# All eight gate columns of the first attention branch ahead of the attention stream

## What is computed

```python
proj = einsum('bld,de->ble', rmsnorm(x, attn_norm_w), w_in)
a_q, a_k, a_v, i_q, i_k, i_w, b_q, b_k, b_v, g_a, g_b = split(proj)
o_a = dsa_branch(...)      # each query attends to the 128 causal keys that an index picks
o_b = swa_branch(...)      # sliding window of 128 keys, with a sink logit per head
mix = sigmoid(g_a) * (o_a @ w_branch_a) + sigmoid(g_b) * (o_b @ w_branch_b)
x = x + mix @ w_out
```

## Time and profile before

| | us |
|---|---|
| three runs, median | 1595.26 |
| three runs, lowest and highest | 1594.77, 1597.05 |
| the profiled execution, its own time | 1593.72 |
| its span in the trace | 1591.9 |

### The profile page before, as it was taken

How to read it: one execution, slowest core, us unless ns; L and a number is a source line. 1 busy time by engine, 2 the same in 40 slices (tenths; PEclk the granted TensorE clock), 3 DMA queues, 4 the chain that set the end, 5 groups by cost and what they waited for, 6 DMA issues and landing times.

```text
span 1591.9 us, 19579 instructions
## 1 busy us (share of the span) xinstructions
PE 1578.1 (99%) x7590; PEld 1294.2 (81%) x7590; DVE 768.6 (48%) x1106; ACT 506.2 (32%) x749; POOL 709.0 (45%) x273
## 2 busy tenths in 40 slices
PE   9999999999999999999999999999999999999998
PEld 6887788888888988888888887876678988888886
DVE  6701588910165566666104389987573431023203
ACT  3012211210125444344124344237543432124312
POOL 5875189677771344544442002421143244344451
PEclk9999999999999999999999999999999999999999
DMA  6242032232333233233223222231123122323221
GB/s 220 85 133 79 1 112 80 80 129 83 106 106 106 81 105 105 80 105 106 84 101 114 79 82 80 81 79 28 28 106 133 54 81 105 106 80 106 106 88 71
DMA packets 123285, 147.00 MB, mean 92 GB/s; under 512 B 5143, under 2 KB 98375, under 8 KB 123208
## 3 DMA queue, kind: packets, MB, share of 16 engines
q1 hardware_dynamic: 121334, 141.05, 28.2%
q10 hardware_dynamic: 1874, 4.85, 0.9%
HBM read 143.79 MB, written 2.10 MB: 92 GB/s over the span
## 4 chain that ended last, share of the span: by engine, by line
PE 95%; POOL 2%; issue 1%; ACT 1%; DVE 1%; DMA 0%; SPq 0%; DVEq 0%; POOLq 0%; ACTq 0%
PE ps L646 29%; PE ps L647 28%; PE ps L648 28%; PE ps L788 3%; PE ps L865 2%; PE ps L1032 1%; PE ps L1049 1%; POOL w_lo L599 1%; PE ps L853 1%; POOL w_hi L594 1%; PE ps L924 1%; PE ps L886 0%; DMA raw<-in_w_up 0%; POOL spare_lo_out L599 0%; PE ps L826 0%
## 5 line engine op out<-in xcount | busy, mean ns | idle before, releaser
L599 POOL TENSOR_TENSOR w_lo<-raw,w_hi 128x1024 fp32r<-128x1024 f32 x224 | 557.4, 2509 | 714.9 <-ACT w_hi L1094 712.2
L646 PE MATMUL ps<-hT_hi,w_hi 128*128 128x512 f32 (+1 forms) x928 | 355.7, 383 | 0.8 <-POOL w_lo L599 0.5
L647 PE MATMUL ps<-hT_lo,w_hi 128*128 128x512 f32 (+1 forms) x928 | 354.4, 382 | 0.0
L648 PE MATMUL ps<-hT_hi,w_lo 128*128 128x512 f32 (+1 forms) x928 | 354.3, 382 | 0.0
L1094 ACT ACTIVATE w_hi<-raw 128x2048 fp32r<-128x2048 f32 (+1 forms) x87 | 165.0, 1896 | 246.5 <-PE ps L646 212.3
L646 PEld LDWEIGHTS ps<-hT_hi,w_hi 128*128 128x128 f32 x928 | 174.4, 188 | 37.0 <-issue 2.3
L648 PEld LDWEIGHTS ps<-hT_hi,w_lo 128*128 128x128 f32 x928 | 174.4, 188 | 33.7
L647 PEld LDWEIGHTS ps<-hT_lo,w_hi 128*128 128x128 f32 x928 | 174.5, 188 | 33.5
L594 POOL TENSOR_TENSOR w_hi<-raw,cells 128x2048 fp32r<-128x2048 f32 x35 | 130.1, 3716 | 127.7 <-PE ps L646 126.0
L648 PE MATMUL ps<-w_hi,f_lo 128*128 128x512 f32 x400 | 155.6, 389 | 0.0
L646 PE MATMUL ps<-w_hi,f_hi 128*128 128x512 f32 x400 | 155.6, 389 | 0.0
(11 more groups left out here) (306 smaller groups left out, 2188.3 us busy)
## 6 DMA issues: line engine op xcount, KB each, us to landing
raw<-in_w_in SPq DMA_DIRECT2D x86, 512.0 KB, 4.6
raw<-in_w_up SPq DMA_DIRECT2D x76, 512.0 KB, 4.6
raw<-in_w_down SPq DMA_DIRECT2D x54, 512.0 KB, 4.1
raw<-in_w_out SPq DMA_DIRECT2D x16, 512.0 KB, 4.3
raw<-in_w_ret_o SPq DMA_DIRECT2D x8, 512.0 KB, 4.1
raw<-in_w_sgu_o SPq DMA_DIRECT2D x8, 512.0 KB, 4.1
x<-in_x SPq DMA_DIRECT2D x4, 512.0 KB, 6.0
raw<-in_w_branch_b SPq DMA_DIRECT2D x4, 512.0 KB, 6.2
```

Source lines behind the costliest of these rows:

```text
L599: nc.gpsimd.tensor_tensor(lo[:, c], raw[:, s, c], hi[:, c].bitcast(f32), ALU.subtract).then_inc(unit_split, 1)
L646: first = nc.tensor.matmul(dst, a_hi, b_hi, start=start, stop=False)
L647: nc.tensor.matmul(dst, a_hi, b_lo, start=False, stop=False)
L648: return first, nc.tensor.matmul(dst, a_lo, b_hi, start=False, stop=stop)
```

## The change

`GA_IN` goes from 7 to 8. So `GA_PARTS` is 0, the stream's first four parts are gone, and the parts of `y_b` are numbered from 0; they stay in the same steps. The eighth `g_a` column is made ahead of the stream and evacuated as a sigmoid. `y_b`'s first unit gets its high part after the sixth sigmoid. The late sigmoid is gone.

```diff
-GA_IN = 7
+GA_IN = 8
...
-HI_AT = {1: U0["y_b"], GA_PARTS + 1: U0["y_b"] + 1, GA_PARTS + 9: U0["y_a"]}
+HI_AT = {1: U0["y_b"] + 1, 9: U0["y_a"]}
...
             for j in range(GA_IN // 2):
                 unit_T(U0["g_a"] + j, T0["g_a"] + 2 * j, KT, 256, hT_hi, hT_lo)
-            column(U0["g_a"] + 3, G_A[6], KT, 256, 0, hT_hi, hT_lo)
...
                 evacuate(G_A[c], sig_a[:, c, :], ACT.Sigmoid)
-                if c in (1, 3):
+                if c in (1, 3, 5):
                     give_hi(U0["g_a"] + c // 2 + 2, started=True)
...
-            nc.scalar.activation(sig_a[:, GA_IN:KT, :], sig_a[:, GA_IN:KT, :], ACT.Sigmoid).then_inc(sigmoids_made, 1)
             give_hi(U0["y_a"] + 1, started=True)
```

## The result

The changed kernel takes **1600.87 us** in the median of 12 runs (1596.60 to 1602.13), the kernel before 1595.98 in 12 (1594.19 to 1597.60): a ratio of 1.0029, interval 1.0021 to 1.0036. It is slower by 0.3%, some 4.9 us. The forecast was 1595.7 and the range ended at 1599.5: it missed, on the side of rivals A and B.

The account below looks back on a forecast made before the run. TensorE, busy 99% of the span, was taken to bound the kernel. The terms 5.44 - 5.52 - 1.2 + 1.7 gave +0.4 us on the median of 1595.26, so 1595.7; the range ran from 1593.2 to 1599.5.

Parts of the forecast that it names:

- A: Rival: VectorE and ScalarE pace the stream, so TensorE gains nothing from the missing parts; 1599.5 to 1600.7, chance 0.09.
- B: Rival: the granted clock falls in the stream without its dense parts; +7.5, about 1603, chance 0.05.
- Point 1: Ahead of the stream: the eighth column's 24 dense matmuls add 5.44 us on TensorE, hidden by nothing.
- Points 2 to 4: In the stream: four dense parts leave, -5.52 us; GpSimd's low part leaves, -1.2; new waits, +1.7.
- Point 3: Step 9: GpSimd's low part no longer holds VectorE's addition, -1.2 us; two rotations ahead are held, with 1.6 to spare.
- Point 4: In the stream: without the parts as cover, TensorE newly waits for VectorE and ScalarE; +1.7 us, bounds 0 and 5.5.
- Point 5: Late sigmoid, its table load, ScalarE's column copy, moved high part and SP's earlier load cost nothing.
- The clock: Steps 0 to 14: granted clock stays at 1.00, the 2.4 GHz level, as in steps 15 to 22.
- C: Rival: two steps of lead absorb all new waits in the stream; -1.3 us, 1594.0, chance 0.22.
- D: Rival: the changed kernel is faster by more than 3.2 us, through an unseen effect; chance 0.03.
- The signs: Changed profile: first mask operation to step 12's transposes 23.5 us, rotations end before 1069, PEclk stays 1.00.

Follow-up runs that it names:

- a_dense2: Changed kernel with six more dense matmuls (512 columns, result unused) at the end of step 2; 1597.88 us, ratio 1.0018.
- a_trans2: Changed kernel with ten more transposes of 128 columns at the end of step 2; 1596.94 us, ratio 1.0013.
- a_exp: Changed kernel with the exponential's table loaded during the eighth column, which is copied, its sigmoid made after the stream; 1594.89 us, ratio 0.9995.
- b_exp: Kernel before with the exponential's table loaded early, during the seventh column; 1594.11 us, ratio 0.9989.
- a_wait4: Changed kernel with four dense matmuls (result unused) inside TensorE's 1.0 us wait for the first exponential; 1595.94 us, ratio 1.0002.
- b_no2: Kernel before with the first of the stream's four dense parts moved from step 2 to step 15; 1595.54 us, ratio 1.0002.
- a_again: Changed kernel run once more with no edit; 1600.01 us, ratio 1.0027.
- a_dense10: Changed kernel with six more dense matmuls (512 columns, result unused) at the end of step 10; 1598.56 us, ratio 1.0026.
- b_no2_e24: b_no2 with 24 dense matmuls (result unused) ahead of the seventh column, the wait for the exponential kept; 1604.07 us, ratio 1.0054.

## Why the prediction failed

**Point 1, the 24 matmuls ahead: right.** No wait and no changed pace appeared ahead of the stream; they cost what the earlier trace rows say.

**Points 2 to 4, the stream with the clock up: right in sum.** It is 55.7 us (a_dense2, a_trans2 without their fill) against 60.57, a gain of 4.9; forecast were 5.52 + 1.2 - 1.7 = 5.0. So the change without the fall costs +0.5, where I had +0.4. A second reading, free of the wait: a_exp and b_exp have streams of 55.14 and 59.59, so 5.44 - 4.45 = +1.0; the median of a_wait4 says the same, 1.1 above the kernel before. The sum was off by 0.1 to 0.7 us, and the rest of the 4.9 is the fall.

**Point 3, GpSimd's low part: right.** TensorE's step 9, and what happened ahead of the stream on VectorE:

```profile
1089.14 0.63 PE L788 MATMUL ps<-ident,probs 128*128 128x128 f32 x4
...
1090.96 0.63 PE L788 MATMUL ps<-ident,probs 128*128 128x128 f32 x4
...
1093.41 0.66 PE L788 MATMUL ps<-ident,probs 128*128 128x128 f32 x4
...
1095.96 0.41 PE L788 MATMUL ps<-ident,probs 128*128 128x128 f32 x2
```

```profile
1062.37 2.80 DVE L1574 TENSOR_TENSOR rope_u<-qn,rope 128x512 f32<-128x512 f32 x1
1065.09 2.88 DVE L1575 TENSOR_TENSOR rope_u<-qn,rope 128x512 f32<-128x512 f32 x1
...
1069.27 0.29 DVE L1582 TENSOR_TENSOR kn<-rope_u 128x128 f32<-128x128 f32 x1
1071.17 0.35 DVE L1875 CUSTOM_DVE_ANT_0 probs<-ps,band,cells 128x128 f32<-128x128 f32 x1 [1.61 <-PE ps L1031]
```

Step 9 takes 1.82 us where it took 3.00. Two rotations are held, as expected, and the 1.61 us that VectorE then waits for the logits is the spare time of 1.6 that the prediction worked out.

**Point 4, new waits: right in sum, each part off.** The list of waits doesn't show them, the distances do. From the transposes of step 11 to those of step 12 it is 1095.96 - 1093.41 = 2.55 us, against 1.85 for a plain step: 0.7, forecast 0.8. Step 8 comes 2.32 after step 7 (forecast 0.2 above plain, measured 0.5), and step 16 takes 2.77 where it took 2.23 before (0.5, forecast 0.2). In the early steps I forecast 0.5; with the wait removed (a_exp) a step takes 2.18 where a free one takes 1.95, so 0.2. Sum 1.9, forecast 1.7.

**Point 5: nothing speaks against it**; the late sigmoid's going showed nowhere.

**"The clock": this is the step that failed.** The prediction let, steps 15 to 22 at 1.00, speak for steps 0 to 14, and noted that those have fewer columns and more gaps, then gave that no weight: the clock stood in the sum at nothing, and its fall cost some 4 of the 4.9 us. The rows were of a stretch without a wait. Steps 0 to 5 follow a wait of 1.0 us, and TensorE had come to that wait from short logits matmuls. The dense part of step 2, which I priced as six matmuls and some cover for waits, had another side: put back alone (a_dense2) it goes with a PEclk of 1.00 and a stream of 57.1 us instead of 61.0. It isn't the whole cause, since the kernel before mostly keeps its clock without it (b_no2). The wait is the surer one: with it gone (a_exp) or filled (a_wait4) the clock stays.

**The rivals.** B named the mechanism, at 0.05, and sized it wrongly: a fall through all of the 50 us at the price of logits matmuls alone, +7.5. The falls seen behind the wait of 1.0 us are 3.3 to 14 us long and cost 0.4 to 0.5 us for each, some 5 in a_again. Per matmul B was too low: four logits matmuls took 1077.96 - 1076.80 = 1.16 us at the low level, 0.29 each, where it had 0.213, and the transposes, which it left out, slowed as well. The rule on transposes that pointed to B isn't borne out by a_trans2, so B's coming true in part doesn't speak for that reason. A is refuted by a_wait4 and a_exp, where the same chains on VectorE and ScalarE run and the time is that of the kernel before. C is refuted: with the clock up there are new waits of 1.9 us, and the change costs +0.5 to +1.0 where C had -1.3. D never came near.

**The signs.** From the first mask operation to the transposes of step 12 it takes 1095.96 - 1071.17 = 24.8 us, forecast 23.5. Step 3 alone, at the low level, is 1077.96 - 1074.75 = 3.21 for the 1.95 that it takes in a_trans2; that is 1.26 of the 1.3. The rotations ended at 1069.56, not before 1069, as the execution began 1.3 us late. PEclk gave the verdict.

## What to carry to other kernels

Before filler work is taken out of a sparse stretch, look at what lies right ahead of the place: a wait of even 1 us followed by short matmuls is where the granted clock fell here, and a few matmuls or transposes there came with a shorter time in spite of their own cost (a_dense2, a_trans2). Better still, remove the wait, as by loading ScalarE's table one evacuation early; then the filler isn't needed. And when several executions of one kernel scatter by more than their neighbour's, look at each one's mean clock before any profile is explained: the one profiled may be the exception. A median and a trace that disagree, as in a_dense10, say that it is.

## What the runs showed of the hardware

- Behind a wait of 1.0 us on TensorE, with steps of 128 and 256-column matmuls after it, the granted clock went to 0.50 (1.2 GHz) in the middle of a kernel in which TensorE was busy 99% of the span. It stayed there for 3.3 us (after), 10 (b_no2_e24), 13.5 (a_again) or 14 (a_dense10) and came back by itself in the same kind of steps. In seven traces without the wait it stayed up.
- With ten transposes of 128 columns (1.26 us) behind the wait the clock stayed up, as with six matmuls of 512 columns (1.64 us).
- Whether it falls also depends on where the stream lies in time: a mean clock of 0.997 or less in one execution of 11 in one place, in five of five when the same steps came a column later. This is unexplained.
- VectorE operations with two operands from SBUF are held beside GpSimd's low part in more than one size: rotations of 512 elements took 2.80 and 2.88 us (0.69 for the same kind alone), as those of 128 took 2.51 and 2.37.
